# Two attention blocks of a diffusion-style network rebuilt, and a convolution done in place, on one Trainium2 core

## The reference, cut to what matters

```python
# SSD: depthwise convolution of width 5, then silu, then the scan
xbc = jax.nn.silu(dwconv(xbc, conv_w, conv_b))

# even: 8 heads of 64; latent queries see the latent (with a bias table) and the context,
# context queries see the context alone
s_loc = q @ k_lat * d**-0.5 + bias
s_ctx = q @ k_ctx * d**-0.5
p = softmax(concat(s_loc, s_ctx)); o = p @ v

# odd, window part: 8 query heads, 2 key heads, a band mask, a sink in the denominator
# odd, diff part: 4 heads of two softmax maps each
a = softmax(q1 k1) - lam * softmax(q2 k2); o = a @ v
yd = rms_norm_2(yd, subln_g) * (1.0 - lam_init)

# before both: every head of q and k is normalised (rms over its 64 features, times a gain);
# in odd, latent q and k are turned by rope
q = rms_norm_2(split_heads(q), q_g)
```

## Time and profile before

| | |
|---|---|
| median of three runs | 3602.71 us (3601.45 to 3604.27) |
| profiled execution | 3605.16 us, of which the span is 3603.4 us |
| PE busy | 3213.0 us, 89% of the span |
| DVE busy | 1328.3 us, 37% |
| ACT busy | 557.3 us, 15% |
| mean granted TensorE clock | 0.919 of full speed |

### The profile page before, as it was taken

One profiled execution on the slowest core, in us unless ns is written; L12 is line 12 of the kernel. 1 busy time (PEld: TensorE's weight loads), 2 busy tenths in 40 slices (PEclk: granted clock), 3 DMA queues, 4 the chain that ended last, 5 costly groups with the idle time before them and its releaser, 6 DMA issues.

```text
span 3603.4 us, 31613 instructions
## 1 busy us (share of the span) xinstructions
PE 3213.0 (89%) x12574; PEld 2029.4 (56%) x12574; DVE 1328.3 (37%) x3165; ACT 557.3 (15%) x1077; POOL 0.2 (0%) x4
## 2 busy tenths in 40 slices
PE   7996889999987877899997779999999666999999
PEld 2446344444565555688743344444455335799998
DVE  2655365477426566411210433533010553001011
ACT  1111110000214334120100321000011222100000
POOL 0000000000000000000000000000000000000000
PEclk9998889999988988899998779999999657999999
DMA  7530145565241111145313002543322002478885
GB/s 247 181 128 1 46 152 187 152 188 189 70 117 47 38 33 47 61 151 150 117 70 87 1 1 94 187 136 105 96 85 91 0 0 71 169 252 289 278 269 204
DMA packets 382833, 431.46 MB, mean 120 GB/s; under 512 B 15257, under 2 KB 291384, under 8 KB 382554
## 3 DMA queue, kind: packets, MB, share of 16 engines
q1 hardware_dynamic: 281840, 329.77, 27.9%
q10 hardware_dynamic: 100842, 99.62, 8.6%
HBM read 428.32 MB, written 1.05 MB: 119 GB/s over the span
## 4 chain that ended last, share of the span: by engine, by line
PE 80%; DVE 11%; ACT 3%; issue 3%; DVEq 1%; DMA 1%; ACTq 0%
PE bank L813 48%; PE bank L2178 9%; PE bank L830 5%; PE bank L2192 4%; PE bank L838 4%; PE bank L1753 2%; PE bank L517 2%; PE bank L1746 1%; DVE arena L1475 1%; DVE small L1800 1%; PE bank L2160 1%; DVE uT L1798 1%; ACT L1455 1%; PE bank L2204 1%; DVE arena L1505 1%
## 5 line engine op out<-in xcount | busy, mean ns | idle before, releaser
L813 PE MATMUL bank<-uT,slot 128*128 128x512 f32 (+2 forms) x2848 | 1071.6, 535 | 2.1 <-DVEq L2364 2.1
L813 PEld LDWEIGHTS bank<-uT,slot 128*128 128x128 f32 (+1 forms) x2848 | 539.2, 191 | 480.9 <-issue 455.4
L813 PE MATMUL bank<-arena,slot 128*128 128x512 f32 (+1 forms) x2016 | 695.7, 507 | 30.6 <-DVEq L2364 30.6
L813 PEld LDWEIGHTS bank<-arena,slot 128*128 128x128 f32 x2016 | 387.7, 194 | 318.8 <-issue 279.0
L560 DVE SCALAR_TENSOR_TENSOR arena<-arena,sT 128x256 f32<-128x256 f32 x784 | 333.7, 481 | 8.0
L2178 PE MATMUL bank<-arena,slot 128*128 128x128 f32 x2816 | 317.6, 276 | 5.1 <-issue 4.4
L2178 PEld LDWEIGHTS bank<-arena,slot 128*128 128x128 f32 x2816 | 316.7, 193 | 7.9 <-issue 7.8
L886 DVE SCALAR_TENSOR_TENSOR hT<-bank,mod,hT 128x256 f32<-128x256 f32 (+1 forms) x104 | 41.6, 439 | 419.2 <-PE bank L813 419.2
L830 PE MATMUL bank<-uT,slot 128*128 128x512 f32 (+1 forms) x448 | 168.5, 541 | 24.4 <-ACT uT L582 12.5
L2263 DVE TENSOR_TENSOR arena<-bank,halves 128x256 f32<-128x256 f32 (+1 forms) x48 | 19.3, 403 | 435.6 <-ACT halves L2224 435.6
L2192 PE MATMUL bank<-slot,arena 128*128 128x256 f32 x704 | 153.3, 379 | 1.0 <-DVEq L144 1.0
(11 more groups left out here) (295 smaller groups left out, 2458.1 us busy)
## 6 DMA issues: line engine op xcount, KB each, us to landing
arena<-in_ada_w ACTq DMA_DIRECT2D x88, 1024.0 KB, 5.2
slot<-in_ffn_w SPq DMA_DIRECT2D x42, 2048.0 KB, 8.9
slot<-in_moe_w SPq DMA_DIRECT2D x32, 2048.0 KB, 10.4
slot<-in_moe_w SPq DMA_DIRECT2D x32, 1408.0 KB, 8.8
slot<-in_moe_w SPq DMA_DIRECT2D x16, 1536.0 KB, 9.2
slot<-in_gla_w_in SPq DMA_DIRECT2D x6, 2048.0 KB, 10.3
slot<-in_ev_w_in SPq DMA_DIRECT2D x6, 2048.0 KB, 8.0
slot<-in_ffn_w SPq DMA_DIRECT2D x8, 1408.0 KB, 6.8
```

What stands on the lines that cost most here:

```text
L813: ins = pe.matmul(bank[0:m, 0:t1 - t0], w[:, k, c0:c0 + m], x[:, k, t0:t1], start=(k == 0), stop=(k == kt - 1))
```

## The change

Bias, mask and scores are now summed by TensorE in the bank; the maximum and the exponential read the bank; the division moves to the output copy; the output comes out token-major and is turned afterwards ("f" products); window and diff items of the odd mixer alternate; head norms, rope, the bias flips, the doubled keys and lambda stand between the projection tiles; `SubNorm` becomes a square with row sum per item. In the scan the convolution writes straight into the tile that silu then works on in place, and the four silus of a group stand together.

New helpers and the even projection:

```diff
+        def head_square(act, x, n, T):
+            act.wait_ge(*S("head").taken("act"))
+            act.activation(rl[n % 2][:, 0:T], x, ACT.Square).then_inc(*S("squares").given())
+        def head_sum(pe, B, i, n, T):
+            pe.wait_ge(*S("squares").taken("pe"))
+            bank = B.empty(pe, i)
+            pe.matmul(bank[:, 0:T], half, rl[n % 2][:, 0:T], start=True, stop=True).then_inc(full_sem, 1)
+        def head_scale(dve, B, i, n, x, gain, T):
+            r = rstd_wait(dve, n, T)
+            B.release(dve, i)
+            dve.scalar_tensor_tensor(out=x, in0=x, scalar=vc(gain), in1=r, op0=ALU.mult, op1=ALU.mult)\
+               .then_inc(*S("rstd_used").given())
...
         class EvenProject(Stage):
...
+            def __init__(self):
+                order = [("q", j) for j in range(4)]
+                for j in range(4):
+                    order += [("k", j), ("sum", j)]
+                for j in range(4):
+                    order += [("b", j), ("sum", 4 + j)]
+                for j in range(4):
+                    order += [("c", j), ("flip", 2 * j), ("flip", 2 * j + 1)]
+                order += [("u", j) for j in range(4)] + [("v", j) for j in range(4)]
+                order = [ev for ev in order if ev[0] != "flip" or ev[1] < len(self.FLIPS)]
+                self.order, self.index = order, {ev: i for i, ev in enumerate(order)}
...
+                    elif kind == "sum":
+                        head_sum(pe, B, i, j, TOK)
+                    elif kind == "flip":
+                        raw, _, heads, c = self.FLIPS[j]
+                        if j == 0:
+                            pe.wait_ge(S("moe_loads").sem, 16 * 16)
...
+                        pe.matmul(bank[:, 0:src.shape[1]], const[:, C_FLIP:C_FLIP + P], src, start=True,
+                                  stop=True).then_inc(full_sem, 1)
...
+                    for raw, first, heads in m_braw:
+                        for h in range(heads):
+                            src = bass.AP(tensor=t.tensor, offset=(first + h) * 15 * 31 + (5 - b) * 31 + 15 - 63,
+                                          ap=[[1, GRID], [31, 6], [1, GRID]])
+                            act.dma_start(raw[64 * b:64 * b + 64, h, :, :], src).then_inc(S("moe_loads").sem, 16)
+                for n in range(2):
+                    head_square(act, self.head(n)[0], n, TOK)
+                for i, (kind, j) in enumerate(self.order):
+                    if kind == "sum":
+                        rstd_act(act, B, ch, j, i, TOK, 64, RMS_EPS)
+                        if j + 2 < 8:
+                            head_square(act, self.head(j + 2)[0], j + 2, TOK)
```

The attention stage and its items:

```diff
         class Attention(Stage):
...
+            def __init__(self, items, turns, ahead):
+                self.items, self.turns, self.ahead = items, turns, ahead
+                self.maps = list(itertools.accumulate(len(it["maps"]) for it in items))
+                N, order = len(items), []
+                for n in range(-ahead, N + 2):
+                    if n + ahead < N:
+                        order += [("s", n + ahead, j) for j in range(len(items[n + ahead]["maps"]))]
+                    if 0 <= n < N:
+                        order += [("t", n, 0)]
+                    if 0 <= n - 1 < N:
+                        order += [("o", n - 1, 0)]
+                    if n - 2 in turns:
+                        order += [("f", n - 2, 0)]
...
             def pe(self, pe, B):
...
+                        q, k = it["maps"][j]
+                        if it["bias"] is None:
+                            pe.matmul(bank[:, 0:nk], q, k, start=True, stop=True).then_inc(full_sem, 1)
+                        else:
+                            pe.matmul(bank[:, 0:LAT], ident, it["bias"], start=True, stop=False)
+                            pe.matmul(bank[:, 0:LAT], q, k[:, 0:LAT], start=False, stop=True)
+                            pe.matmul(bank[:, LAT:nk], q, k[:, LAT:nk], start=True, stop=True).then_inc(full_sem, 1)
...
+                        two = len(it["maps"]) == 2
+                        pe.wait_ge(*S("pn" if two else "pr").taken("pe"))
+                        S("pr").passed("pe", 2 if two else 0)
...
+                    elif kind == "o":
+                        B.freed(pe, self.order["t", n, 0])
+                        bank = B.empty(pe, i)
+                        w = it["v"][0].shape[1]
+                        for t, v in enumerate(it["v"]):
+                            ins = pe.matmul(bank[:, 0:w], m_pt[n % 2][:, t * P:t * P + P], v, start=(t == 0),
+                                            stop=(t == len(it["v"]) - 1))
...
+                        for t, x in enumerate(src):
+                            ins = pe.transpose(bank[:, t * P:t * P + P], x, ident)
...
             def act(self, act, B, ch):
...
+                    if n + self.ahead < N:
+                        it = self.items[n + self.ahead]
+                        for j in range(len(it["maps"])):
+                            mx, nm, den, es = self.stats(n + self.ahead, j)[0:4]
+                            i = self.order["s", n + self.ahead, j]
+                            act.wait_ge(*S("nm").taken("act"))
+                            if it["sink"] is not None:
+                                act.activation(es, sinks[:, it["sink"]:it["sink"] + 1], ACT.Exp, bias=nm)
+                            s = self.score(n + self.ahead, j)
+                            act.activation(s, B[i][:, 0:it["nk"]], ACT.Exp, scale=0.125, bias=nm,
+                                           accum_out=den).then_inc(*B.free(i))
+                            act.drain().then_inc(*S("pr").given())
+                    if 0 <= n - 1 < N and self.items[n - 1]["sub"]:
+                        i, (ssq, f) = self.order["o", n - 1, 0], self.stats(n - 1, 1)[4:6]
+                        eps = self.stats(n - 1, 0)[5]
+                        bank = B.full(act, i)
+                        act.activation(m_turned[:, 0:P], bank[:, 0:P], ACT.Square, accum_out=ssq)
+                        ch.wait(ch(act.drain()))
+                        ch.wait(ch(act.activation(f, ssq, ACT.Ln, scale=1.0 / P, bias=eps)))
+                        act.activation(f, f, ACT.Exp, scale=-0.5).then_inc(*S("root").given())
...
             def dve(self, dve, B, ch):
...
+                        for j in range(len(it["maps"])):
+                            mx, nm = self.stats(n + self.ahead, j)[0:2]
+                            bank = B.full(dve, self.order["s", n + self.ahead, j])
+                            dve_link(ch, dve.tensor_reduce(mx, bank[:, 0:it["nk"]], AX.X, ALU.max))
+                            if it["sink"] is not None:
+                                ins = dve.tensor_scalar(nm, mx, -0.125, sinks[:, 8 + it["sink"]:9 + it["sink"]], ALU.mult,
+                                                        ALU.min)
+                            else:
+                                ins = dve.tensor_scalar(nm, mx, -0.125, None, ALU.mult)
+                            ins.then_inc(*S("nm").given())
+                        if len(it["maps"]) == 2:
+                            (den, _, rc, eps), (den1, _, rc1, _) = (self.stats(n + self.ahead, j)[2:6] for j in range(2))
+                            s0, s1 = (self.score(n + self.ahead, j) for j in range(2))
+                            dve.wait_ge(pr, before + self.maps[n + self.ahead])
+                            dve.scalar_tensor_tensor(out=eps, in0=den, scalar=RMS_EPS, in1=den, op0=ALU.mult, op1=ALU.mult)
+                            dve_link(ch, dve.reciprocal(rc1, den1))
+                            dve_link(ch, dve.tensor_scalar(rc, den, rc1, lam_t, ALU.mult, ALU.mult))
+                            dve.scalar_tensor_tensor(out=s0, in0=s1, scalar=rc, in1=s0, op0=ALU.mult,
+                                                     op1=ALU.add).then_inc(*S("pn").given())
+                    if 0 <= n - 1 < N:
+                        it, i = self.items[n - 1], self.order["o", n - 1, 0]
+                        den, es, rc = self.stats(n - 1, 0)[2:5]
+                        w = it["v"][0].shape[1]
+                        if it["sub"]:
+                            dve.wait_ge(*S("root").taken("dve"))
+                            rc = self.stats(n - 1, 1)[5]
+                        else:
+                            dve.wait_ge(pr, before + self.maps[n - 1])
+                            if it["sink"] is not None:
+                                dve_link(ch, dve.tensor_tensor(den, den, es, ALU.add))
+                            dve_link(ch, dve.reciprocal(rc, den))
+                        dve.tensor_scalar(it["o"], bank[:, 0:w], rc, None, ALU.mult).then_inc(*B.free(i))
...
+                        if gain is None:
+                            ins = dve.tensor_copy(dst, bank[:, 0:P * len(src)])
+                        else:
+                            ins = dve.tensor_scalar(dst, bank[:, 0:P * len(src)], gain, None, ALU.mult)
```

(43 more changed lines are left out.)

528 lines of the change are left out of this document (229 added, 299 removed).

## The result

The changed kernel takes 3380.2 us (median of 4 runs, 3376.9 to 3386.7) against 3603.5 us: a ratio of 0.938, 95% interval 0.937 to 0.940. The forecast was 3428 us with a range from 3385. The profiled execution took 3381.7 us with a span of 3379.9.

What follows compares the result with a forecast made beforehand. TensorE, with 80% of the chain, was taken to bound the kernel, idling and losing clock in attention. Savings 27 + 46 + 24 + 55 + 22 = 174 us off 3605.2 gave 3431, as a median 3428 us; range 3385 to 3485.

Steps and rivals of the forecast that it cites:

- rival 4: Both attentions: all gaps vanish and the odd chain hides behind TensorE, 20 and 30 us less, 3378 us; chance 0.04.
- rival 3: Projections: TensorE's clock falls there too as small products wait; slower than before, 3632 us at a third; chance 0.02.
- three changes 0.15 each: Even attention, latent item: three changes of 0.15 us each on TensorE, within 3.3 us an item.
- 10.5 us for filling, clock and tail: Even attention: 4.5 us for filling, 3 for first items at the lower clock, 3 for the tail, within 94.5.
- no gaps: Even attention: lower bound of the whole stage, 74 us.
- Rival 1: Both attentions: clock keeps falling, half the time at the lower level, 117 and 135 us, kernel 3473; chance 0.20.
- price of the lower level, 155 us: Even attention: stage time at the lower clock throughout, 6.2 us a latent and 2.9 us a context item.
- (b): Odd attention, out of the diff item: output, maximum and its negative, sink and exponential, hops, 3.4 us.
- (c): Odd attention, window to next item: TensorE's turns, the diff item's output and the next scores, 3.8 us.
- 12 us for fill, tail and lower clock: Odd attention: 7 us for fill and tail, 5 for stretches at the lower clock, on top of eight cycles' 101.
- (a): Odd attention, into the diff item: turns, copy, two exponentials, the join and six hand-overs, 5.0 us.
- 22 us in all: Scan: batching four silus leaves 16 table changes and saves 3 us a group, 22 in all, bounds 0 and 33.

Runs made afterwards that it cites:

- even_sums_last: Kernel after, with the even projection's eight sums of squares behind its last tile instead of between the tiles: 3413.2 us.
- sums_before_v: Kernel after, with the even projection's eight sums of squares together ahead of its four last tiles: 3387.7 us.
- both_late: Kernel after with odd attention's scores two items ahead, plus the even attention's bias and division passes on VectorE from the ninth item on: 3378.1 us.
- division_on_map: Kernel after, with the even attention's division made by VectorE on the map ahead of the turns, not at the output copy: 3432.8 us.
- bias_on_vector: Kernel after with odd attention's scores two items ahead, plus latent and window items' bias added by VectorE instead of a TensorE product: 3408.2 us.
- idle_before_even: Kernel after, with the first product of the even attention held back by eight ScalarE copies: 3382.9 us.
- even_one_ahead: Kernel after, with the even attention's scores one item ahead instead of two: median 3417.2 us.

## Why the forecast was too high

What the change does was forecast rightly, stage by stage; the sizes of several terms were not, and two carried most of the miss of 48 us (49.5 between the profiled executions): even attention 21, odd attention 13.5. Scan and projections together were 4 off (5 too much, 9 too little), and 11 lie outside of the terms, some 5 of them chance. That the time stands 2 us from rival 4 (3378, chance 0.04) is partly luck: its even attention came, 21 us less for its 20, but its odd chain did not hide behind TensorE (13.5 us less for its 30, with 14.5 us of waiting left), and the 11 us that no term has make up most of the difference.

**Even projection and odd projection** went by their steps: TensorE busy for 178.5 of 179.2 and 115.2 of 116.0 us, 0.99 and 0.98 of full clock. The changes of stationary operand, 0.2 and 0.15 us each, were 3.0 and 4.4 us of the sums; without them most of the miss of 4.1 and 4.7 us is gone. The earlier trace rows did not bear them out: its gaps before turns are 1.17 and 1.88 us, both waits for VectorE's division, and none is near 0.2. That the tiles hide the heads is shown by the 7.5 us of even_sums_last; rival 3 has nothing for it.

**Even attention, failed step: "three changes 0.15 each", and 10.5 us for filling, clock and tail.** TensorE's instructions in one cycle of two latent and two context items:

```profile
1954.68 0.65 PE L1763 MATMUL bank<-arena,const 128*128 128x256 f32 x2
1955.27 0.70 PE L1764 MATMUL bank<-arena 64*128 64x256 f32 x2
1955.80 0.59 PE L1765 MATMUL bank<-arena 64*128 64x256 f32 x2
1956.33 0.44 PE L1772 MATMUL bank<-const,uT 128*128 128x128 f32 x2
1956.60 0.56 PE L1779 MATMUL bank<-arena,uT 128*128 128x64 f32 x4
...
1963.41 0.43 PE L1763 MATMUL bank<-arena,const 128*128 128x256 f32 x1
```

The first starts follow each other by 0.59, 0.53, 0.53, 0.27 us: an operand changes without a gap, and where a length reaches past the next start the two overlap. The three score products take 1.65 us against 1.31 in the sum, four turns 0.49 against 0.66 and the output 0.84 against 0.89. A latent item is 2.98 us from start to start, 0.12 more than its products were priced at, not 0.45. The cycle is 1963.41 - 1954.68 = 8.73 us against 10.1 in the forecast; eight cycles make 11 of the 20.6 us of the miss. The other 9.7 are filling, turning products, clock and tail: 4.0 us were left for them where I had 13.7, of which 3 were for first items at the lower clock; the clock was 1.00 from the first. The stage lies at the lower bound, 74 us with "no gaps".

The likeliest value was no good choice for a deeper reason. I took a middle between the bounds, as if the stage ran a little slower everywhere. The runs show long stretches at one level: with the same instructions the stage takes 73.9 us (after, sums_before_v) or, in the profiled run of even_sums_last, 109.8. Values in between do occur (87.7 us in both_late, 108.4 in division_on_map); they depend on where the clock falls and when it comes back. Rival 1 had the right mechanism and missed how abrupt it is: a fall at some place and then a long stay, with TensorE busy all the time. That its 117 us are the time of bias_on_vector is a coincidence; that run spent nearly the whole stage at the lower level, with less work, where rival 1 has half of the time there. Its price of the lower level, 155 us, was too high: at the 222 instructions in 69.0 us that even_sums_last does at 0.50, the 433 of the stage would take some 135, an estimate.

The kernel after starts this stage behind a dense projection, and its first items have no wait over 0.2 us except the one at its start. Four runs fit the reading that this keeps its clock (idle_before_even, even_sums_last, bias_on_vector, division_on_map); both_late does not, since it fell 50 us later without a wait over 0.65 us. By even_sums_last the head norms between the tiles earn more than the time of their own stage. The rule of the Trainium skill ("TensorE: Matmul & The Clock Gate", A second HAM failure mode: psum-queue depth-cycling), that small idle times between groups of products make the clock swing, fits the odd attention of after, where the clock falls behind every second join and comes back. It does not cover the even stage of bias_on_vector and division_on_map: there the clock did not swing back between bursts, but stayed low for 70 us and more.

What made the even attention of before slow is narrowed down, not told apart. Its 38.9 us of waiting are gone in after. With the passes removed and the distance of one item kept (even_one_ahead) 4.3 us of it are left and the stage takes 79.0 us where the clock holds; two of the four runs were some 40 us longer. With the distance of two, one pass back from the ninth item on makes the stage 5.7 us quicker or 1.5 us slower; one back from the first item on, or both from the ninth, lost the clock. So each of the two edits takes most of the waiting away by itself (2.6 us of waits for the division in both_late); the clock held where both stand for the first eight items and at least one pass stays away from there on. No run has both passes back at the distance of one, or both from the first item.

**Odd attention, failed step: parts (b) and (c) of the chain, and 12 us for fill, tail and lower clock.** The way through the join was the right one, and the eight waits show it. TensorE's turns in one cycle at full clock (diff, window, window, diff), and the scores of the diff item:

```profile
2712.04 0.66 PE L1772 MATMUL bank<-const,uT 128*128 128x128 f32 x4 [1.15 <-DVE uT L1843]
...
2715.01 0.66 PE L1772 MATMUL bank<-const,uT 128*128 128x128 f32 x4
...
2716.49 1.13 PE L1761 MATMUL bank<-arena 64*128 64x512 f32 x4
2717.55 0.66 PE L1772 MATMUL bank<-const,uT 128*128 128x128 f32 x4
...
2722.65 0.66 PE L1772 MATMUL bank<-const,uT 128*128 128x128 f32 x4 [2.05 <-DVE uT L1843]
```

The three steps are 2.97, 2.54 and 5.10 us, 10.6 in all, for (b) 3.4, (c) 3.8 and (a) 5.0 with 0.4 for the turning products. Most of the difference in (c) is that the four instructions of the two maps' scores take 1.06 us from start to start, where I had 4 x 0.433: two of them, for one map of the same size, take 1.05 us (both_late, starts at 1982.48 and 1983.53). The two maps lie on different halves of the partitions, and here the second costs nothing. A cycle with a slow stretch takes 13.3 us. The joins stand 23.9 us apart for two cycles, 12.0 for one against the 12.6 of the sum: 5 us. Filling, tail and slow stretches were put at 12 us on top. The slow stretches are inside the 12.0 (every second cycle has one, 2.7 us each), and 4 us are left for the rest: 8 us. What I did not see at all is that the order of the kinds costs 9 us at this distance, and the distance itself 25.

**Scan, mis-sized: 22 us in all.** The 3 us a group were nearly right: a group is now 49.9 us (starts of its first products at 1117.20, 1167.11, 1217.01) against 52.7, 2.8 less. But not every group gives it, and over the scan it is 16.9. The first gives 2.0, and the one from 1316.95 on 0.5: the 16 instructions of its first tile take 9.3 us at a mean clock of 0.76, where they take 7.0 at 1.00 in the group before. ScalarE around the batch, and the product that waits for it:

```profile
1149.99 0.63 ACT L1461 ACTIVATE arena<-arena 128x512 f32<-128x512 f32 x1 [4.35 <-DVE arena L1505]
...
1150.64 1.28 ACT L1443 ACT_TABLE_LOAD   x1
...
1151.93 1.95 ACT L1443 ACTIVATE arena<-arena,vectors 128x512 f32<-128x512 f32 x3
...
1152.11 0.70 PE L1419 MATMUL bank<-arena 128*64 128x128 f32 x4 [5.03 <-DVE arena L1521]
```

Two of three loads have left the chain; a wait of 5.0 us stays, now for VectorE (L1521) where it was for ScalarE. Ahead of it in VectorE's queue stands the convolution, which the change did not move. The Trainium skill ("ScalarE: Activation LUTs", What ACT_TABLE_LOAD costs) adds a drain of 1380 ns to each change of set; here the Exp ends at 1150.62, the load runs from 1150.64 to 1151.92 and the silu starts at 1151.93, so the trace does not agree.

## What to carry to other kernels

Price a stage at full clock and at the lower one, and give the likelihood to the two and not to a mean: in the even attention the time was set by where the clock fell and how long it stayed down. Look at the waits among the first items and at the end of the stage ahead before you take work off an engine: an edit that takes 7 us of work off TensorE cost 43 us when it opened a wait at the start, and gained its full 5.7 us when it began eight items later. That is no safe rule, since two such edits together lost the clock in the middle of the stage. When an engine waits for a chain of other engines, try one more item of lookahead before removing instructions from the chain; one changed argument gave 20 us.

## What the runs showed of the hardware

A TensorE that is busy for 9.03 of 9.03 us can stand at a granted clock of 0.50 for 70 us (division_on_map) or for 110 us to the end of the stage (bias_on_vector) while 433 instructions of the same kind run at 1.00 in other kernels. In rows, "busy" beside 0.50 is little more than half of the progress: 33 instructions against 55 in 9.03 us. A single gap of 2.8 us did not lower the clock (idle_before_even), while single waits of 1.1 and 1.2 us inside the first items were followed by the fall, and in both_late it fell behind waits of at most 0.65 us. The level at the entry does not decide it: the row ahead of the stage stands at 1.00 in even_sums_last too. Why the clock comes back in division_on_map and even_sums_last after so long, and not before the end of the stage in bias_on_vector and both_late, the runs don't settle; nor do they show what sets apart gaps of so different an effect. Score products of two maps on different halves of the partitions overlap: four instructions of 512 columns in 1.06 us, two in 1.05. even_one_ahead sits on the edge: two runs of 3391 and 3398 us, two of 3436 and 3439.
